# First and third sum of weight blocks made on GpSimd and VectorE instead of by accumulating transfers

## What is computed

```python
h = modulate(rms_norm(x, norm_g[i, j]), shift, scale)
x = x + 0.5 * gate * swiglu(h, ffn_w_gu[i, j], ffn_w_down[i, j])   # D_FF = 2816
```

## Time and profile before

| | |
|---|---|
| runs | median 2807.55 us (2794.46 to 2811.48) |
| profiled execution | 2811.35 us, span 2809.7 us |
| TensorE (PE) busy | 2717.4 us, 97% of the span |
| VectorE (DVE) busy | 1961.8 us, 70% |
| ScalarE (ACT) busy | 1236.9 us, 44% |
| GpSimd (POOL) busy | 403.0 us, 14% |
| mean granted TensorE clock | 0.982 |
| chain that ended last | PE 83%, DVE 9%, ACT 3%, issue 3% |
| DMA | 382.82 MB, mean 136 GB/s |

### The profile page before, as it was taken

The page is one execution under the profiler, slowest core; times in us unless marked ns, Lnnn a source line. Parts: engine busy times, 40 slices in busy tenths (PEclk is TensorE's granted clock), DMA queues, the critical chain, the costliest instruction groups (busy, mean ns, idle before and its releaser), DMA issues.

```text
span 2809.7 us, 49345 instructions
## 1 busy us (share of the span) xinstructions
PE 2717.4 (97%) x19483; PEld 2337.9 (83%) x19483; DVE 1961.8 (70%) x3036; ACT 1236.9 (44%) x2061; POOL 403.0 (14%) x504
## 2 busy tenths in 40 slices
PE   8999888999999999999999999999999999999998
PEld 7855777887888878888889999899998866799997
DVE  4587553666777555555359888798897876498886
ACT  3355443333333233222255455564554265464553
POOL 1000110112000111011121111211112300211111
PEclk8899999999999999999999999999999999999999
DMA  6331000674222555556437777477674310277673
GB/s 239 113 99 63 6 3 10 216 234 135 96 98 92 178 165 180 187 198 192 130 92 180 184 170 182 122 180 186 174 179 116 110 33 29 72 185 181 170 182 91
DMA packets 133114, 382.82 MB, mean 136 GB/s; under 512 B 16432, under 2 KB 26416, under 8 KB 132784
## 3 DMA queue, kind: packets, MB, share of 16 engines
q1 hardware_dynamic: 82480, 256.22, 27.8%
q0 software_dynamic: 50432, 123.76, 20.2%
HBM read 376.77 MB, written 2.10 MB: 135 GB/s over the span
## 4 chain that ended last, share of the span: by engine, by line
PE 83%; DVE 9%; ACT 3%; issue 3%; POOL 1%; DMA 1%; SPq 0%; POOLq 0%; DVEq 0%; ACTq 0%
PE psum L2594 12%; PE psum L2596 12%; PE psum L2595 12%; PE psum L2755 9%; PE psum L2757 9%; PE psum L2756 9%; DVE w_lo L1712 2%; PE psum L2882 1%; PE psum L2884 1%; PE psum L2883 1%; PE psum L3385 1%; PE psum L3396 1%; POOL rexp L803 1%; DVE hid_lo L1819 1%; PE psum L2857 1%
## 5 line engine op out<-in xcount | busy, mean ns | idle before, releaser
L1569 DVE TENSOR_TENSOR w_lo<-stage,w_hi 128x1024 fp32r<-128x1024 f32 (+2 forms) x261 | 297.7, 1141 | 326.5 <-ACT w_hi L935 326.4
L935 ACT ACTIVATE w_hi<-stage 128x1024 fp32r<-128x1024 f32 (+2 forms) x261 | 258.5, 991 | 508.0 <-PE psum L2596 460.4
L2594 PE MATMUL psum<-h_hi,w_hi 128*128 128x512 f32 (+1 forms) x1064 | 417.7, 393 | 3.5 <-DVE w_lo L1569 2.6
L2595 PE MATMUL psum<-h_lo,w_hi 128*128 128x512 f32 (+1 forms) x1064 | 416.1, 391 | 0.0
L2596 PE MATMUL psum<-h_hi,w_lo 128*128 128x512 f32 (+1 forms) x1064 | 416.0, 391 | 0.0
L2755 PE MATMUL psum<-h_hi,w_hi 128*128 128x256 f32 x960 | 270.1, 281 | 7.1 <-DVE w_lo L1712 7.1
L2757 PE MATMUL psum<-h_hi,w_lo 128*128 128x256 f32 x960 | 268.7, 280 | 0.0
L2756 PE MATMUL psum<-h_lo,w_hi 128*128 128x256 f32 x960 | 268.3, 280 | 0.0
L1048 ACT ACTIVATE w_hi<-stage 128x1024 fp32r<-128x1024 f32 (+1 forms) x192 | 192.9, 1005 | 149.0 <-PE psum L2757 124.5
L2755 PE MATMUL psum<-hid_hi,w_hi 128*128 128x256 f32 x840 | 238.3, 284 | 11.2 <-issue 10.7
L1712 DVE TENSOR_TENSOR w_lo<-stage,w_hi 128x1024 fp32r<-128x1024 f32 (+1 forms) x192 | 221.5, 1154 | 34.2 <-ACT w_hi L1048 32.7
(11 more groups left out here) (521 smaller groups left out, 6345.9 us busy)
## 6 DMA issues: line engine op xcount, KB each, us to landing
stage<-in_up SPq DMA_DIRECT2D x208, 512.0 KB, 4.1
mod_w<-in_mod_w POOLq DMA_DIRECT2D x144, 512.0 KB, 4.0
stage<-in_up POOLq DMA_DIRECT2D x120, 256.0 KB, 4.3
stage<-in_down SPq DMA_DIRECT2D x40, 512.0 KB, 4.2
stage<-in_down SPq DMA_DIRECT2D x48, 384.0 KB, 3.5
mod_w<-in_up SPq DMA_DIRECT2D x60, 256.0 KB, 3.9
stage<-in_down SPq DMA_DIRECT2D x32, 448.0 KB, 3.4
stage<-in_w_in SPq DMA_DIRECT2D x24, 512.0 KB, 3.4
```

What stands on the lines that cost most here:

```text
L935: act.activation(w_hi[:, c % 2, 0:kt * cols], stage[:, at % NSTAGE, 0:kt * cols], ACT.Copy).then_inc(hi_done, 1)
L1569: dve.tensor_tensor(w_lo[:, c % 2, 0:kt * cols], stage[:, place[c] % NSTAGE, 0:kt * cols], w_hi[:, c % 2, 0:kt * cols].bitcast(F32), ALU.s ...
L2594: pe.matmul(dst, wh[:, n], a_hi[:, k], start=start and n == 0, stop=False)
L2595: pe.matmul(dst, wh[:, n], a_lo[:, k], start=False, stop=False)
```

## The change

The array in HBM holds four blocks a group: w11, w21, w12, w22. Slot b is loaded with w12 alone. s1 is a GpSimd addition of `a22_buf` into slot a, after both have landed. s3 is a VectorE subtraction, s2 - w22, written into slot b's second half. The addition for s4 moves, in VectorE's loop, from behind low part s2 (G+1) to behind low part q (G), after s3's. Both accumulating transfers are gone.

```diff
--- before.py
+++ after.py
@@ -381,8 +381,8 @@
         st_prod = sem("st_prod")
         st_hi, st_lo, st_s2 = sem("st_hi"), sem("st_lo"), sem("st_s2")
         st_a22 = [sem("st_a22_0"), sem("st_a22_1")]
-        st_s1_in = [sem("st_s1_in0"), sem("st_s1_in1")]
-        st_s3_in = [sem("st_s3_in0"), sem("st_s3_in1")]
+        st_s1 = sem("st_s1")
+        st_s3 = sem("st_s3")
         st_s4 = sem("st_s4")
         st_snap, st_silu = sem("st_snap"), sem("st_silu")
         st_row1, st_c22, st_mult = sem("st_row1"), sem("st_c22"), sem("st_mult")
@@ -710,7 +710,7 @@
                 for e in range(2):
                     q = place[f, G, e]
                     slot_free(sp, q)
-                    sp.dma_start(stage[:, q % NSTAGE, 0:2 * n], w[:, 2 * n * e:2 * n * (e + 1)]).then_inc(loaded[q % NSTAGE], 16)
+                    sp.dma_start(stage[:, q % NSTAGE, 0:(2 - e) * n], w[:, 2 * n * e:n * (e + 2)]).then_inc(loaded[q % NSTAGE], 16)
                 if G >= 2:
                     sp.wait_ge(st_lo, split_of(f, "q", G - 2))
                 elif f > 2:
@@ -719,7 +719,7 @@
                     sp.wait_ge(unit_done, seg["attn_out"].first + 1)
                 if f == 2 and G < 2:
                     sp.wait_ge(mod_done, 2 * MOD_TILES)
-                sp.dma_start(a22_buf[G % 2][:, 0:n], w[:, 4 * n:5 * n]).then_inc(st_a22[G % 2], 16)
+                sp.dma_start(a22_buf[G % 2][:, 0:n], w[:, 3 * n:4 * n]).then_inc(st_a22[G % 2], 16)
 
             for s in seg.values():
                 if s.name == "mix_in":
@@ -869,26 +869,17 @@
 
                 n, q = group_kp(G) * P, place[f, G, 0]
                 pool.wait_ge(loaded[q % NSTAGE], 16 * (q // NSTAGE + 1))
-                pool.dma_start(stage[:, q % NSTAGE, n:2 * n], group_source(f, G)[:, 4 * n:5 * n],
-                               accum_op=ALU.add).then_inc(st_s1_in[G % 2], 16)
-
-            def sum_s3(f, G):
-
-                n, q = group_kp(G) * P, place[f, G, 1]
-                pool.wait_ge(loaded[q % NSTAGE], 16 * (q // NSTAGE + 1))
-                pool.dma_start(stage[:, q % NSTAGE, n:2 * n], group_source(f, G)[:, n:2 * n],
-                               accum_op=ALU.add).then_inc(st_s3_in[G % 2], 16)
+                pool.wait_ge(st_a22[G % 2], 16 * (before(f, NG // 2) + G // 2 + 1))
+                pool.tensor_tensor(stage[:, q % NSTAGE, n:2 * n], stage[:, q % NSTAGE, n:2 * n], a22_buf[G % 2][:, 0:n],
+                                   ALU.add).then_inc(st_s1, 1)
 
             def ffn(f, n_norm):
 
                 sum_s1(f, 0)
-                sum_s3(f, 0)
                 sum_s1(f, 1)
-                sum_s3(f, 1)
                 for G in range(NG):
                     if G + 2 < NG:
                         sum_s1(f, G + 2)
-                        sum_s3(f, G + 2)
                 for k in range(KD):
                     gather(n_norm + 1, k)
 
@@ -1027,8 +1018,10 @@
                     if name in ("a", "b"):
                         q = place[f, G, "ab".index(name)]
                         act.wait_ge(loaded[q % NSTAGE], 16 * (q // NSTAGE + 1))
-                        act.wait_ge((st_s1_in if name == "a" else st_s3_in)[G % 2],
-                                    16 * (before(f, NG // 2) + G // 2 + 1))
+                        if name == "a":
+                            act.wait_ge(st_s1, before(f, NG) + G + 1)
+                        else:
+                            act.wait_ge(st_s3, before(f, NG) + G + 1)
                         if G:
                             act.wait_ge(st_prod, step_of(f, "P5" if name == "a" else "P7", G - 1))
                         else:
@@ -1716,17 +1709,26 @@
 
                     n, q = group_kp(G) * P, place[f, G, 0]
                     dve.wait_ge(loaded[q % NSTAGE], 16 * (q // NSTAGE + 1))
-                    dve.wait_ge(st_s1_in[G % 2], 16 * (before(f, NG // 2) + G // 2 + 1))
+                    dve.wait_ge(st_s1, before(f, NG) + G + 1)
                     if G >= 2:
                         dve.wait_ge(st_lo, split_of(f, "s4", G - 2))
                     dve.tensor_tensor(s2_buf[G % 2][:, 0:n], stage[:, q % NSTAGE, n:2 * n], stage[:, q % NSTAGE, 0:n],
                                       ALU.add).then_inc(st_s2, 1)
 
+                def sum_s3(G):
+
+                    n, q = group_kp(G) * P, place[f, G, 1]
+                    dve.wait_ge(st_a22[G % 2], 16 * (before(f, NG // 2) + G // 2 + 1))
+                    dve.wait_ge(st_s2, before(f, NG) + G + 1)
+                    dve.tensor_tensor(stage[:, q % NSTAGE, n:2 * n], s2_buf[G % 2][:, 0:n], a22_buf[G % 2][:, 0:n],
+                                      ALU.subtract).then_inc(st_s3, 1)
+
                 def sum_s4(G):
 
                     n, q = group_kp(G) * P, place[f, G, 1]
                     dve.wait_ge(loaded[q % NSTAGE], 16 * (q // NSTAGE + 1))
                     dve.wait_ge(st_lo, split_of(f, "s2", G))
+                    dve.wait_ge(st_s3, before(f, NG) + G + 1)
                     dve.tensor_tensor(s2_buf[G % 2][:, 0:n], s2_buf[G % 2][:, 0:n], stage[:, q % NSTAGE, 0:n],
                                       ALU.add).then_inc(st_s4, 1)
 
@@ -1867,6 +1869,7 @@
                 part_lo("a", 0)
                 dif_low(1)
                 part_lo("s2", 0)
+                sum_s3(0)
                 sum_s4(0)
                 dif_low(2)
                 plain_hid(1)
@@ -1900,7 +1903,6 @@
                         into_x(G, "12")
                     if G + 1 < NG:
                         part_lo("s2", G + 1)
-                        sum_s4(G + 1)
                     if G == 0:
                         dif_low(3)
                     if G and late == "u":
@@ -1914,6 +1916,9 @@
                             hid_low(x, p)
                     if G < NG:
                         part_lo("q", G)
+                    if G + 1 < NG:
+                        sum_s3(G + 1)
+                        sum_s4(G + 1)
                     for x, p in hid_early(G):
                         if x == "B":
                             hid_low(x, p)
@@ -3494,7 +3499,7 @@
 
     rows = w[2 * first * P:2 * (first + count) * P, 2 * out * P:2 * (out + 1) * P].reshape(count, 2, P, 2, P)
     block = {(i, k): rows[:, k, :, i].transpose(1, 0, 2).reshape(P, count * P) for i in range(2) for k in range(2)}
-    return np.concatenate([block[0, 0], block[1, 0], block[0, 1], block[0, 0], block[1, 1]], axis=1)
+    return np.concatenate([block[0, 0], block[1, 0], block[0, 1], block[1, 1]], axis=1)
 
 
 def columns(x):
```

## The result

The changed kernel took 2980.24 us (median of 4 runs) against 2808.89 us of the kernel before on the same chip (4 runs, 2794.46 to 2811.48). The ratio is 1.0625, 95% interval 1.0584 to 1.0666: 171 us slower, where 2918 us was forecast with a range up to 2955. (The median counts one run of 10366.74 us, with a granted clock of 0.562; the ratio leaves it out, and the median of the other three, 2975.02 to 2981.17, is 2979.31.) The profiled execution took 2981.17 us, span 2979.5. From the end of the first P1 to the end of the last P1 (group 31) the three FFNs took 351.1, 349.8 and 350.1 us instead of 294.7, 292.5 and 296.8: 167.0 of the 169.8 us that the span grew.

What follows compares the result with a forecast made beforehand. TensorE was taken to bound the kernel before. 38.5 us per FFN, 115.5 for three, less 5 for the vanished stall gave +110.5: 2921.9 us for the profiled execution, 2918 us for the median, range 2865 to 2955.

Steps and rivals of the forecast that it cites:

- the ring: Once per group: q's low part, a22 load, GpSimd's addition, s2 sum, VectorE's queue; 12.09 us late "g", 11.47 late "u".
- S to q and b's low part: VectorE, s2 sum's start to q's low part's end: 6.95 and 6.80 us; b's low part ends 3.92 and 3.45 later.
- GpSimd's turn: GpSimd's s1 addition takes turns with VectorE's low part of b and ends 1.12 us after it.
- The landing, 2.7 us: The a22 load lands 2.7 us after issue (2.3 for 192 KB), with 3.9 kept as the upper end.
- a22 lands late: Rival: the a22 load takes 3.9 us, some 0.5 us more per group in 17 groups; +30, 2948 us; chance 0.15.
- It binds in 17 groups, 1.95 us each: Up groups of each FFN, less the two following a down group and the last, cost 33.2 us together.
- Three runs of groups use up slack: -3: In each FFN, three runs of groups first use up slack of about 1 us each, leaving 30 us.
- The down groups, +1.5 and +7: Per FFN, 1.5 us more for the four down groups of 4 pairs and 7 us for those of 3 pairs.
- The stall that goes, -5: At 2658.55, the wait for an accumulated block vanishes: 3.5 us of stall and 1.5 of slow matmuls.
- hidden: Rival: the wait for s1 is hidden and the transfer stall goes; 2802 us, faster; chance 0.09.
- no turns: Rival: GpSimd and VectorE run side by side, +1.28 us per group; +68, 2875 us; chance 0.20.
- clock: Rival: after new stalls TensorE runs at low clock 8 us per group and is the bound again; 3000 us; chance 0.06.

Runs made afterwards that it cites:

- e6: Changed kernel with SyncE waiting for w22's landing before issuing the next two loads; 10 us less by the ratio, 16 in the FFNs alone.
- e1: Changed kernel with w22 also loaded early into slot b for both sums, a22_buf only for q; 2880 us, 82 over the kernel before.
- e9: Changed kernel with GpSimd's s1 addition made twice; 135 us more than the changed kernel from S to S over 93 groups.
- e14: Kernel before with VectorE's s3 subtraction only in groups 8 to 11 and 18 to 21; 2789.37 us, ratio 0.9979.
- e5: Changed kernel with three filler matmuls ahead of P3 in up groups and P6 in down groups; 6 us lower by the ratio.
- e2: Changed kernel with s1 as an accumulating transfer again, s3 still VectorE's subtraction; 2836 us, 39 over the kernel before.
- e10: Changed kernel with w22 loaded early into slot b and s1 added by VectorE ahead of s2's sum; 101 us over the kernel before.
- e13: Changed kernel with s1 added by VectorE and SyncE waiting for w22's landing before the next two loads; 2908.77 us, ratio 1.0402.

## Why the prediction was wrong

The starts of the s2 sum (S) from group to group, after minus before, in us. The step of group G runs from S(G) to S(G+1), and the sums over steps 0 to 30 are those of the FFNs from P1 to P1:

```
steps                                  forecast per FFN   FFN 1   FFN 2   FFN 3
17 up groups (0-6, 12-16, 22-26)          33.2 - 3         34.2    34.6    33.6
4 down groups of 4 pairs (7-10)            1.5              6.1     7.3     7.9
7 down groups of 3 pairs (17-20, 28-30)    7 (2 in FFN 3)   9.3    10.5     5.3
3 up groups not charged (11, 21, 27)       0                6.8     4.8     6.6
sum                                       38.5 (33.5)      56.4    57.3    53.4
```

What failed is the term of the sum for the groups in which the ring adds time. It was put at 38.5 us per FFN: 17 up groups less 3 for slack, 1.5 for the down groups of 4 pairs, 7 for those of 3, nothing for three up groups. The runs show 57.3 us in the second FFN, with nothing hidden.

**The bound now and the mechanism: right.** The ring closed as told: issue 0.03 us behind q, GpSimd, S with VectorE idle ahead of it, TensorE's stall at P3.

**S to q and b's low part: right.** S to q is 7.14 and 6.89 us (forecast 6.95 and 6.80), b's low part ends 3.96 and 3.50 us behind q (3.92 and 3.45).

**GpSimd's turn: right in half of the groups.** With late "g" the addition starts about when b's low part ends, and S comes at q + 5.24 (forecast 5.14): the turn's arm, though w22 lands there only shortly before. In e6, where it lands well before, S still comes at q + 5.20, with the addition's end 1.15 us behind b's low part, where the forecast had 1.12. The Trainium skill (SBUF — State Buffer, section Who interferes with whom) has a VectorE instruction with two SBUF inputs and a GpSimd instruction that reads SBUF exclude one another; the additions of e6 and the 52 us of VectorE time in e1 agree.

**The landing, 2.7 us: wrong, and the smaller part.** It is 3.6 us in steady up groups and 3.0 alone, so late "u" has S at q + 5.19 instead of 4.67, and in the down groups of 4 pairs it is the longer arm as well. A steady pair is 24.5 us instead of 23.56. The rival "a22 lands late" had this mechanism and gave it 30 us; shortening the landing by 0.5 gave 10 to 16, and brought S of late "u" to q + 4.78.

**"It binds in 17 groups, 1.95 us each": the sum near by luck, the number of groups wrong.** They cost 34.1 us in the mean for 33.2. But the twelve steady steps (1 to 6, 14, 15, 23 to 26) cost 2.3 us each (the late landing is most of the difference), and the other five (0, 12, 13, 16, 22) only 1.2. And the two up groups behind a round, which were to catch up, and the last one, whose next w22 is small, cost 6 us more per FFN, 18 in all. e9 shows it from the other side: an additional 1.36 us costs 1.45 in the mean of all 93 groups.

**"Three runs of groups use up slack: -3": failed.** In the second FFN steps 1 to 5 cost 12.1 us by S and 10.1 by P1, so 2 us of slack did give. In steps 6 and 7 P1 lost 7.3 where S lost 4.9: the slack was a loan. Over the whole FFN both counts give 57.3.

**The down groups, +1.5 and +7: the +1.5 failed.** Four groups of 4 pairs cost 7.1 us in the mean, those of 3 pairs 9.9 in the first two FFNs. "TensorE's pace is 9.97, the ring 10.5" was made for a steady group with the quick landing; no row was shown for the 10.5, and in the kernel before the four steps took 11.2, 9.4, 9.9 and 10.0. Timeline of VectorE around S in the down groups of four pairs:

```profile
1990.70 0.69 DVE L1715 TENSOR_TENSOR mod_w<-stage 128x512 f32<-128x512 f32 x1 [1.94 <-issue]
...
1995.77 0.69 DVE L1705 TENSOR_TENSOR w_lo<-mod_w,w_hi 128x512 fp32r<-128x512 f32 x1 [0.24 <-ACT w_hi L1041]
...
2001.74 0.69 DVE L1715 TENSOR_TENSOR mod_w<-stage 128x512 f32<-128x512 f32 x1 [1.48 <-POOL stage L873]
...
2013.36 0.69 DVE L1715 TENSOR_TENSOR mod_w<-stage 128x512 f32<-128x512 f32 x1 [2.06 <-POOL stage L873]
```

11.0 and 11.6 us from S to S: S to q is 5.75, q to S 5.3 and 5.9. The step that enters the down groups (7) took 13.6 us from S to S (11.2 before). The forecast priced no such edge, and let part of the 0.5 us per group vanish in slack that VectorE, late by the ring, did not have.

**The stall that goes, -5: right.** The stretch of P1 that held it (third FFN, groups 18 to 21) grew by 1.0 us, the same stretch of the other two by 4.3 and 5.4, and the third FFN lost 3 to 4 us less. The ring's stalls stand in its place, so the profile shows no gain there. e14 shows it alone, 4.9 us.

The sum over three FFNs: up groups 102.4 - 90 = 12.4, down groups of 4 pairs 21.3 - 4.5 = 16.8, of 3 pairs 25.1 - 16 = 9.1, the three groups not charged 18.2, outside the FFNs 2.8: 59.3 us, which is what lies between the 169.8 us that the span grew and the forecast's 110.5. No price of an engine's operation was far off; the landing's was, and e6 gives 16 us in the FFNs for 0.5 of its 0.9. The larger part is where the ring was taken to bind, and how much of it slack would hide. The three other rivals: "hidden" and "no turns" fell with S at q + 5.2; "clock" had the time nearly right (3000) for a reason that e5 refutes, with 92 us at the low level whose removal gave 6.

What stays open: how the 44 us between e2 and e1 divide between longer VectorE operations and later copies on ACT, and why e10's second operation is dearer than the first. How the 43 us or so that e6 leaves of the miss divide between the edges of the rounds and the slack is read from the steps, and no run took one of them away alone.

## What to carry to other kernels

A load that may start only when a buffer is freed, and whose data the first instruction of the next round needs, closes a ring: sum its arms and take the longer. Then set it against the old pace of every kind of round, the short ones and the edges too, with no deduction for slack unless something lets the chain catch up. An engine that is 90% busy in an in-order queue can have no room: one more 0.69 us operation cost nearly its whole length in the up groups. And stalls plus lost clock adding up to the loss prove nothing; take the suspected cost away (a filler, another source) and see whether the time follows.

## What the runs showed of the hardware

- From issue to landing, a 256 KB load of w22 with nothing issued behind it until it had landed took 2.8 to 3.5 us (medians 3.1 in e6, 2.9 in e13; 192 KB 2.3), and 3.1 to 4.5 (median 3.6) in the changed kernel, where another load was issued 0.4 us later.
- GpSimd's 128x512 addition took 1.28 to 1.30 us when it began behind VectorE's low part of b. When it began while that ran, it ended 1.13 to 1.16 us behind it in 62 of 63 cases of e6, and took up to 2.2 us there. VectorE's 128x512 subtraction was 688 ns in the mean in e2 and 763 in e1.
- After most stalls of some 2 us (1.77 in the timeline above) TensorE's clock was granted at 0.5 for a few us, 92 us in the FFNs; with the stalls filled it never fell there.
